# Writing feed-forward inputs tile by tile inside the preceding projection, with parameters loaded once and layers written out

## The reference, cut to what matters

```python
for l in range(2):                                          # first stack
    x = x + 0.5 * swiglu(rms_norm(x, ffn1_norm[l]), ...)    # "ffn1"
    h = rms_norm(x, mix_norm[l]); ...                       # convolutions, sparse attention ("mix1")
    x = x + concat(y_a, y_b, y_c) @ w_out[l]
    x = x + cross_attention(rms_norm(x), rms_norm(mem))     # "xat", ends in a projection by xa_wo
    x = x + 0.5 * swiglu(rms_norm(x, ffn2_norm[l]), ...)    # "ffn2"
x = rms_norm(x, final_norm)
for l in range(2):                                          # second stack
    x = x + concat(y_a, y_b, y_c) @ w_out[l]                # latent attention, GLA, retention ("mix2")
    h = rms_norm(x, ffn_norm[l]); u = h @ ffn_w_up[l]       # "ffn3", D_FF = 2816
    x = x + (silu(conv3(u[..., :D_FF])) * u[..., D_FF:]) @ ffn_w_down[l]
x = rms_norm(x, final_norm_2)
```

## Time and profile before

| what | value |
|---|---|
| median of 3 runs | 4199.54 us |
| the runs | 4196.47 to 4202.67 us |
| span of the profiled execution (first to last instruction) | 4204.2 us |
| mean granted clock of PE over the span | 0.918 |
| PE busy | 3739.8 us (89%) |
| POOL busy | 2541.1 us (60%) |
| DVE busy | 2078.3 us (49%) |
| ACT busy | 864.4 us (21%) |

### The profile page before, as it was taken

The page is one execution under the profiler, slowest core; times in us unless marked ns, Lnnn a source line. Parts: engine busy times, 40 slices in busy tenths (PEclk is TensorE's granted clock), DMA queues, the critical chain, the costliest instruction groups (busy, mean ns, idle before and its releaser), DMA issues.

```text
span 4204.2 us, 50324 instructions
## 1 busy us (share of the span) xinstructions
PE 3739.8 (89%) x16864; PEld 3030.7 (72%) x16864; DVE 2078.3 (49%) x3347; ACT 864.4 (21%) x1461; POOL 2541.1 (60%) x1081
## 2 busy tenths in 40 slices
PE   6999686989999999866998999787899989689998
PEld 5887564877887888654777888665778777467877
DVE  5322997534322332699544332365566435555652
ACT  2110114322110110112332110122233112122320
POOL 5887561347887887645334887452278767117876
PEclk9999885999999999976899999896899999779999
DMA  3332220323332333221041333221023223002332
GB/s 103 99 97 88 73 71 11 104 57 90 95 103 83 95 97 102 74 74 42 31 130 49 96 95 103 85 69 31 26 90 95 93 97 98 25 12 90 95 95 85
DMA packets 91483, 330.83 MB, mean 79 GB/s; under 512 B 12848, under 2 KB 13520, under 8 KB 90832
## 3 DMA queue, kind: packets, MB, share of 16 engines
q1 hardware_dynamic: 85456, 320.62, 24.6%
q10 hardware_dynamic: 5888, 8.40, 0.8%
HBM read 318.48 MB, written 2.10 MB: 76 GB/s over the span
## 4 chain that ended last, share of the span: by engine, by line
PE 73%; DVE 15%; issue 8%; ACT 2%; DMA 1%; POOL 1%; DVEq 0%; ACTq 0%; POOLq 0%; SPq 0%
PE banks L468 23%; PE banks L470 23%; PE banks L469 23%; DMA w_raw<-mid 1%; DVE bias L1287 1%; DVE best L1283 1%; DVE square_sum L586 1%; PE banks L815 1%; PE banks L1466 1%; DVE diagonals L1217 1%; DVE diagonals L1215 1%; DVE h_lo L633 1%; DVE diagonals L1213 1%; PE banks L660 1%; POOL w_lo L486 1%
## 5 line engine op out<-in xcount | busy, mean ns | idle before, releaser
L483 POOL TENSOR_TENSOR w_hi<-w_raw,one 128x1024 fp32r<-128x1024 f32 (+2 forms) x524 | 1072.8, 2047 | 1595.7 <-PE banks L470 1417.9
L486 POOL TENSOR_TENSOR w_lo<-w_raw,w_hi 128x1024 fp32r<-128x1024 f32 (+2 forms) x524 | 1427.3, 2724 | 41.2
L468 PE MATMUL banks<-h_hi,w_hi 128*128 128x512 f32 x3216 | 1276.3, 397 | 64.1 <-DVE h_lo L765 35.3
L469 PE MATMUL banks<-h_lo,w_hi 128*128 128x512 f32 x3216 | 1264.8, 393 | 0.0
L470 PE MATMUL banks<-h_hi,w_lo 128*128 128x512 f32 x3216 | 1263.9, 393 | 0.0
L468 PEld LDWEIGHTS banks<-h_hi,w_hi 128*128 128x128 f32 x3216 | 609.6, 190 | 218.7 <-DVE h_lo L765 37.7
L470 PEld LDWEIGHTS banks<-h_hi,w_lo 128*128 128x128 f32 x3216 | 610.0, 190 | 131.6
L469 PEld LDWEIGHTS banks<-h_lo,w_hi 128*128 128x128 f32 x3216 | 610.9, 190 | 126.1 <-issue 0.5
L468 PE MATMUL banks<-act_hi,w_hi 128*128 128x512 f32 x1056 | 413.1, 391 | 13.1 <-DVE act_lo L792 7.2
L469 PE MATMUL banks<-act_lo,w_hi 128*128 128x512 f32 x1056 | 412.2, 390 | 0.0
L470 PE MATMUL banks<-act_hi,w_lo 128*128 128x512 f32 x1056 | 411.9, 390 | 0.0
(11 more groups left out here) (335 smaller groups left out, 4042.6 us busy)
## 6 DMA issues: line engine op xcount, KB each, us to landing
w_raw<-gu SPq DMA_DIRECT2D x176, 512.0 KB, 3.6
w_raw<-dn SPq DMA_DIRECT2D x96, 704.0 KB, 4.1
w_raw<-mid SPq DMA_DIRECT2D x130, 512.0 KB, 3.6
w_raw<-up SPq DMA_DIRECT2D x88, 512.0 KB, 3.6
w_raw<-mix SPq DMA_DIRECT2D x64, 512.0 KB, 3.6
qk_swap<-qk_raw ACTq DMA_DIRECT2D x64, 64.0 KB, 2.5
x<-x_in SPq DMA_DIRECT2D x1, 2048.0 KB, 10.0
decay<-consts SPq DMA_DIRECT2D x2, 1024.0 KB, 6.1
```

Source lines behind the costliest of these rows:

```text
L468: pe.matmul(out, w_hi, m_hi, start=start, stop=False, skip_group_check=True)
L469: pe.matmul(out, w_hi, m_lo, start=False, stop=False, skip_group_check=True)
L483: g.tensor_tensor(wh[:, ch.slot, 0:width], raw[:, ch.slot, 0:width], one[:, 0:1].to_broadcast([P, width]), ALU.mult).then_inc(Ring.hi, 1)
L486: g.tensor_tensor(wl[:, ch.slot, 0:width], raw[:, ch.slot, 0:width], f32(wh[:, ch.slot, 0:width]), ALU.subtract).then_inc(Ring.split, 1)
```

## The change

- `add_tiles` takes a function `low(k)` that writes `hl` tile k of the coming block (with `ffn_low`), and calls it one tile behind the addition. `ffn_act` makes `hh` tile k as soon as x tile k is added, ahead of its square. So the pairs are written tile by tile while PE still works on the projection; the first block's are interleaved with its sums.
- To have `hh`/`hl` free, the cross attention's output goes to `qx_hi`/`qx_lo`, and mix2's to new tiles `mix_hi`/`mix_lo`, which lie over dead tiles. PE waits for tile 6 of the projection to be added before a block's first matmul.
- `ffn_pe` orders: gate 0, up 0, totals, gate 1, up 1, spread, loop.
- `p1`, `p2` and `cpar` hold both layers: `p1` is loaded for both at the start, `p2` and `cpar` between the two layers of the first stack.
- The loops over layers are written out in Python on every engine; loops inside a layer stay.

```diff
     def add_tiles(v, add, n, l, low=None):
         for d in range(KD):
             add(d)
-            if d >= 1:
+            if low is not None and d >= 1:
+                low(d - 1)
+            if 1 <= d < KD - 1 or d == KD - 1 and low is None:
                 norm_dve_sum_tile(v, n, l, d - 1)
-        if last:
-            norm_dve_sum_tile(v, n, l, KD - 1)
+        if low is not None:
+            low(KD - 1)
+            norm_dve_sum_tile(v, n, l, KD - 2)
+        norm_dve_sum_tile(v, n, l, KD - 1)
...
-        project(0, 0, 0)
+        for part in range(2):
+            project(part, 0, 0)
         norm_pe_totals(pe, f.norm, l)
-        project(1, 0, 0)
-        norm_pe_spread(pe, f.norm, l)
         for part in range(2):
             project(part, 0, 1)
+        norm_pe_spread(pe, f.norm, l)
...
     def ffn_act(act, f, l, gain, ready, conv):
-        norm_act_squares(act, f.norm, l, x_tile, ready, end=KD - 1)
-        ready(act, KD - 1)
         for k in range(KD):
+            ready(act, k)
             act.activation(hh[:, k, :], x[:, k, :], ACT.Copy, scale=gain(k)).then_inc(f.norm.hi.sem, 1)
-        norm_act_squares(act, f.norm, l, x_tile, ready, first=KD - 1)
+            act.wait_ge(f.norm.sum.sem, f.norm.sum(l, max(k - 1, 0)))
+            act.activation(sq[:, k % 2, :], x[:, k, :], ACT.Square).then_inc(f.norm.sq.sem, 1)
...
-    def ffn_dve(v, f, l, at, gain, conv, half, next_norm, next_l, sum_last=True):
-        for k in range(KD):
-            v.wait_ge(f.norm.hi.sem, f.norm.hi(l, k + 1))
-            v.scalar_tensor_tensor(hl[:, k, :], x[:, k, :], gain(k), f32(hh[:, k, :]), ALU.mult, ALU.subtract)\
-                .then_inc(f.norm.lo.sem, 1)
-        norm_dve_sum_tile(v, f.norm, l, KD - 1)
+    def ffn_low(v, f, l, gain, k):
+        v.wait_ge(f.norm.hi.sem, f.norm.hi(l, k + 1))
+        v.scalar_tensor_tensor(hl[:, k, :], x[:, k, :], gain(k), f32(hh[:, k, :]), ALU.mult, ALU.subtract)\
+            .then_inc(f.norm.lo.sem, 1)
+
+    def ffn_dve(v, f, l, at, conv, half, next_norm, next_l, low):
...
             sp.wait_ge(led, len(leads))
-            with sp.Fori(0, L) as l:
-                sp.wait_ge(ffn1.norm.lo.sem, ffn1.norm.lo(l, 0))
-                sp.dma_start(p1[:, :], par1[l, :, :]).then_inc(par1_in.sem, 16)
+            for l in range(L):
+                sp.dma_start(p1[:, l, :], par1[l, :, :]).then_inc(params_in, 16)
+            for l in range(L):
                 stack1_chunks(sp, l, load)
-            with sp.Fori(0, L) as l:
+                if l == 0:
+                    for e in range(L):
+                        sp.dma_start(p2[:, e, :], par2[e, :, :]).then_inc(params2_in, 16)
+                        sp.dma_start(cpar[:, e, :, :], convpar[e, :, :, :]).then_inc(params2_in, 16)
+            for l in range(L):
                 sp.wait_ge(finalnorm.scaled.sem, finalnorm.scaled(0, KD))
                 sp.wait_ge(ffn3.x.sem, ffn3.x(l, 0))
-                sp.dma_start(p2[:, :], par2[l, :, :]).then_inc(par2_in.sem, 16)
-                sp.dma_start(cpar[:, :, :], convpar[l, :, :, :]).then_inc(cpar_in.sem, 16)
...
-            with pe.Fori(0, L) as l:
+            for l in range(L):
                 ffn_pe(pe, ffn1, l, ffn1_at(l))
                 mix1_pe(pe, l)
                 xat_pe(pe, l)
+                pe.wait_ge(wo_x.sem, wo_x(l, KD - 1))
                 ffn_pe(pe, ffn2, l, ffn2_at(l))
             norm_pe(pe, finalnorm, 0)
-            with pe.Fori(0, L) as l:
+            for l in range(L):
                 mix2_pe(pe, l)
+                pe.wait_ge(out2_x.sem, out2_x(l, KD - 1))
                 ffn_pe(pe, ffn3, l, ffn3_at(l))
```

More of the change, by code:

```diff
@@ L130, in program @@
     cols = place("cols", [4])
-    p1 = place("params1", [NPAR1])
-    p2 = place("params2", [NPAR2])
+    p1 = place("params1", [L, NPAR1])
+    p2 = place("params2", [L, NPAR2])
     st = place("stats", [3, 48])
@@ L143, in program @@
     small = place("small", [4, 4])
-    cpar = place("conv_par", [KF, 4])
+    cpar = place("conv_par", [L, KF, 4])
     rt = dg[:, :, :, :].rearrange("p b e c -> p (b e c)")[:, 0:3 * S].rearrange("p (n s) -> p n s", n=3)
@@ L260, in program @@
     top[0] = branch_at
+    mix_hi = place("mix_hi", [KD, S], F32R, at=branch_at)
+    mix_lo = place("mix_lo", [KD, S], F32R, at=branch_at + KD * S * 4)
     qn_hi = place("qn_hi", [MH, S], F32R)
@@ L591, in norm_dve_sum, with add_tiles @@
             norm_dve_sum_tile(v, n, l, k, width)
-    def add_tiles(v, add, n, l, last=True):
+    def add_tiles(v, add, n, l, low=None):
         for d in range(KD):
             add(d)
-            if d >= 1:
+            if low is not None and d >= 1:
+                low(d - 1)
+            if 1 <= d < KD - 1 or d == KD - 1 and low is None:
                 norm_dve_sum_tile(v, n, l, d - 1)
-        if last:
-            norm_dve_sum_tile(v, n, l, KD - 1)
+        if low is not None:
+            low(KD - 1)
+            norm_dve_sum_tile(v, n, l, KD - 2)
+        norm_dve_sum_tile(v, n, l, KD - 1)
     def norm_dve_inverse(v, n, l):
@@ L798, in add @@
                 .then_inc(f.x.sem, 1)
-        add_tiles(v, add, next_norm, next_l, last=sum_last)
+        add_tiles(v, add, next_norm, next_l, low)
     def attention_pe(pe, a, l, emit_score, score_banks, freed, key_tiles, emit_out, emptied):
@@ L1101, in xat_pe @@
             pe.wait_ge(wo_x.sem, wo_x(l, d - 1))
-            column_tile(pe, ch, bank[d % 2][:, :], KD, hh_tile, hl_tile).then_inc(Ring.done, 1)
+            column_tile(pe, ch, bank[d % 2][:, :], KD, lambda k: qx_hi[:, k, :], lambda k: qx_lo[:, k, :])\
+                .then_inc(Ring.done, 1)
     def mix1_act(act, l):
@@ L1205, in out_hi @@
             for e in range(2):
-                act.activation(hh[:, 2 * h + e, :], bank[4 + 2 * (h % 2) + e][:, :], ACT.Copy)\
+                act.activation(qx_hi[:, 2 * h + e, :], bank[4 + 2 * (h % 2) + e][:, :], ACT.Copy)\
                     .then_inc(xat.y_hi.sem, 1)
@@ L1383, in add_cross @@
             v.tensor_tensor(x[:, d, :], x[:, d, :], bank[d % 2][:, :], ALU.add).then_inc(wo_x.sem, 1)
-        add_tiles(v, add_cross, ffn2norm, l, last=False)
+        add_tiles(v, add_cross, ffn2norm, l, lambda k: ffn_low(v, ffn2, l, lambda d: par1_at(l, 4, d), k))
     def mix2_chunk(l, m):
@@ L1839, in add_mix @@
             v.tensor_tensor(x[:, d, :], x[:, d, :], bank[d % 2][:, :], ALU.add).then_inc(out2_x.sem, 1)
-        add_tiles(v, add_mix, ffn3norm, l, last=False)
+        add_tiles(v, add_mix, ffn3norm, l,
+                  lambda k: ffn_low(v, ffn3, l, lambda d: p2[:, l, FN0 + d:FN0 + d + 1], k))
     def ffn1_at(l):
@@ L1909, in _ @@
             act.wait_ge(x_in_sem, 32)
+            act.wait_ge(params_in, 16 * L)
             norm_act(act, memnorm, 0, lambda k: memn[:, k, :], lambda a, k: None, width=M)
[L1911 to L1917 removed]
+            for l in range(L):
+                ffn_act(act, ffn1, l, lambda k: par1_at(l, 0, k),
+                        lambda a, k: a.wait_ge(ffn2.x.sem, ffn2.x(l, k + 1 - KD)), False)
                 mix1_act(act, l)
                 xat_act(act, l)
[L1920 removed]
+                ffn_act(act, ffn2, l, lambda k: par1_at(l, 4, k), lambda a, k: a.wait_ge(wo_x.sem, wo_x(l, k + 1)), False)
             norm_act(act, finalnorm, 0, x_tile, lambda a, k: a.wait_ge(ffn2.x.sem, ffn2.x(L - 1, k + 1)))
             act.wait_ge(finalnorm.scaled.sem, finalnorm.scaled(0, KD))
[L1923 removed]
+            for l in range(L):
                 mix2_act(act, l)
[L1925 to L1926 removed]
+                act.wait_ge(params2_in, 32 * L)
+                ffn_act(act, ffn3, l, lambda k: p2[:, l, FN0 + k:FN0 + k + 1], lambda a, k: a.wait_ge(out2_x.sem, out2_x(l, k + 1)), True)
             norm_act(act, endnorm, 0, x_tile, lambda a, k: a.wait_ge(ffn3.x.sem, ffn3.x(L - 1, k + 1)))
```

89 lines of the change are left out of this document (39 added, 50 removed).

## The result

The changed kernel takes 4212.60 us (median of 7 runs, 4211.55 to 4213.25), the kernel before 4199.42 (7 runs, 4196.47 to 4202.67). The ratio is 1.0031, 95% interval 1.0020 to 1.0042: 13 us slower, where 18 us faster was forecast; the stated range ended at 4197. The profiled execution of the changed kernel took 4211.7 us; its span is 4209.9.

A forecast was written before the change was run, and what follows sets the result against it. Bound taken: PE, 73% of the chain (DVE 15%), standing still at block entries. Terms 15.3 + 1.7 + 1 + 2 - 1 - 1 = 18 us, off the median 4199.54, gave 4181.5 us; range 4161 to 4197.

The forecast's parts named there:

- Parameters: Second stack's layer 1: two loads fewer ahead of the tables, where PE waits 9.22 us for the first chunk; 1 us saved.
- Pairs under the projection, ffn1 and ffn2: Entries of ffn1 (layer 1) and ffn2 (twice): 20.7 us saved less three 1.8 us stalls behind the spread, 15.3 us.
- First block: First ffn1: `h_lo` 0 comes at 35 instead of 40; 3.5 - 1.8 = 1.7 us saved, bounds 0 and 3.
- Cost under the projection: Four projections: DVE's added operations crowd POOL, 0.05 us a chunk for 32 chunks; 1 us lost, bounds 0 and 10.
- Loops: Loops over layers written out on all engines: no fetch stop at the loop end; 2 us saved, bounds 0 and 25.
- Rival 5: Small-operation stages: written-out code saves more, up to 20 us; 4163 us, chance 0.12.
- ffn3: ffn3 in each layer: later start offset by relief, 0 net (3.4 slower to 5.7 faster); clock after PE's wait loses 0.5.
- 1 (PE decides in ffn3): ffn3, both layers: PE sets the pace, 2 x 5.7 us more saved and no clock loss; 4169 us, chance 0.17.
- 2 (the gap behind the spread lowers the clock): After each spread: 1.8 us without matmuls lowers PE's clock, 6 x 1.7 = 10 us given back; 4191.7 us, chance 0.1.
- 3 (ports in the projections): Projections: low and sum push POOL past 5.44 us, PE waits in 32 chunks; 4190 us, chance 0.08.
- 4 (DVE at 12.4 us a tile in ffn3): ffn3: DVE and PE walk at 12.4 us a tile instead of 10.97, 58 us lost; 4239 us, chance 0.06.
- 6: Block entries: pairs still come after the projection because ACT's copy waits for a sum, 11 us lost; 4210 us, chance 0.02.

The follow-up runs named there:

- experiment 1: The changed kernel with 32 unused bytes ahead of `act_hi`; 4184.56 us, ratio 0.9960 to the kernel before.
- experiment 8: The kernel of experiment 1 with the eight low parts written after the projection's last addition, ACT's copies still early; 4216.68 us, ratio 1.0039 to the kernel before.
- experiment 3: The kernel before with only the loops over layers written out; 4197.85 us, ratio 0.9989 to the kernel before.
- experiment 9: The kernel of experiment 1 with the spread moved ahead of up tile 1, behind three projections instead of four; 4171.79 us, ratio 0.9930 to the kernel before.

## Why the prediction was wrong, step by step

**The step that failed** is the one that wasn't in the sum: the part "Parameters" counted what holding both layers saves (two loads, 1 us) and gave nothing to what it moves. It puts 992 bytes ahead of the activations, and that costs 26 us by the count of matmuls, 28 us by experiment 1. No projection in the trace of the kernel before ran at 233.3 ns, but the diff showed that every tile behind `params1` moves; "the same matmul at another address" deserved a term with bounds of its own, and had none. With it the sum would have been -18 + 26 = 8 us slower; 13 was measured, and with the terms as measured below it is -15 + 26 = 11.

The other terms, with experiment 1 (placement mended, 16.5 us faster than the kernel before) as the measure of the rest:

- *Pairs under the projection, ffn1 and ffn2*: 15.3 forecast. The distance between POOL's same splits at both ends of each entry shrank by 4.8, 4.3 and 5.0, together 14.1. Right; experiment 8 confirms the size of an entry. The gap of 0.6 us for `h_lo` 7, the full clock and the six stalls of 1.7 us came as worked out.
- *First block*: 1.7 forecast, 1.9 in the changed kernel. First matmul at 35.31 instead of 40.24. Right.
- *Cost under the projection*: 1 us forecast. With the placement mended POOL's splits keep their distance of 5.44 us in the projections: 0.
- *Parameters' loads*: 1 forecast; PE's wait of 9.22 us is 8.17 in the changed kernel. Right for what it counted.
- *Loops*: 2 forecast, 3.2 measured (0.8 to 8.4). Right. Rival 5 falls. At the loop end of the earlier trace rows, whose 2.80 us of "issue" the term started from, PE's last matmul of layer 0 and its first with weights of layer 1 lie 18.5 us apart before and 17.6 in experiment 3: 0.9 gained.
- *ffn3*: 0 and 0.5 of clock a layer forecast; experiment 1 lost 2.7 and 2.6, between the same two splits of POOL. The later start (3.5 us, forecast 3.4) and the relief in the first two steps (8.97 and 9.15 us instead of 10.01 and 10.78, 2.7 in all; forecast 2.6) were right. What failed is "another 1.2 at the end, where the step from tile 20 to 21 took 12.4": I took a later DVE to find a quieter port there. It found a busier one, since POOL already splits 1408-wide chunks. The step became 17.02, and even with a shorter tile 21 behind it (8.2 us instead of 11.0 to the last `act_lo`) the end lost 1.9 instead of gaining 1.2. The wait was 11.5, not 9.

Measured terms: 14.1 + 1.9 + 0 + 1.05 + 3.2 - 5.3 = 15.0, against 16.5 for experiment 1; the rest is within the spread of the runs.

**The rivals.** 1 (PE decides in ffn3): no, PE waited 11.5 us. 2 (the gap behind the spread lowers the clock): no, 6 gaps of 1.7 us left it at 1.00. 3 (ports in the projections): no. 4 (DVE at 12.4 us a tile in ffn3): no, 10.9 a tile from tile 2 to 20; but its price appeared in one tile, and its place was right. 6: no, the pairs are early. None had the sign for the right reason; 0.08 for slower was too little, as all my cases with that sign came from one kind of cause, waits.

## What to carry to other kernels

Compare the distance between the starts of the same matmul before and after a change, in a stretch without gaps: a difference there is not scheduling. A change that resizes any tile moves all that lie behind it; keep moving and weight tiles a multiple of 128 bytes apart, by rounding each placement up to 128. When one engine's late chain ends a stage, look at what the next stage starts beside it: the spread one projection earlier was worth 3 us a layer in ffn3 (experiment 9), the old order there about 4 more (11), and giving PE a half tile to do in the wait 7 (12).

## What the runs showed of the hardware that was not expected

A 128x512 matmul in this three-product form starts every 226.7 ns when moving tile and weights lie a multiple of 128 bytes apart within the partition, and every 233.3 ns at distances of 32 and 96 (228.9 or 233.3 at 64), at a granted clock of 1.00 in all; why is not shown. At 0 and 96 it holds for either side being the moving one (weights by `h_hi` as `h_hi` by weights). On the whole kernel, with all weights off by 32 (experiment 6, one run), it is 76 us over experiment 1, 1.8%.
